# A two-block network on one core: the first projections' chunks five to eight in three passes of halves, and a ninth place for the experts' weights

## The chip, the cores and the metric

The kernel runs on one core of one Trainium2 chip. The metric is the device time of one execution in microseconds. All activations and weights are float32 in HBM.

## The reference, cut to what matters

The network has a first block (a token mixer and a mixture of experts) and a second one (two layers). The change lies in the first projection of the first block and in what surrounds the experts:

```python
hc = modulate(rms_norm(ctx, norm1_g[l]), csh1, csc1)        # 256 context tokens x 1024
s_f, s_b = context_states(hc @ w_in[l][:, HG_KDIM:3 * HG_KDIM + HG_WIDTH], lbs[l])
hx = modulate(rms_norm(x, norm1_g[l]), sh1, sc1)            # 256 tokens x 1024
x_mix, _, _ = token_mixer(hx @ w_in[l], lbs[l], s_f, s_b, *mix_args)
    # split into q, z_f, z_b, v, g (512 columns each), 3 x 512 for the Hyena branch, 2 x 1024 gate logits
x = x + gt1 * x_mix
x = x + gt2 * hier_moe(modulate(rms_norm(x, norm2_g[l]), sh2, sc2), *moe_args)
    # 32 experts, each with w_up, w_gate (1024 x 512) and w_down (512 x 1024)
```

Each direction of the scan needs log f = log(lb + (1 - lb) * sigmoid(z)), its running sums over chunks of 32 tokens, and several exponentials of them. Then follow two transformer layers of the second block.

## The kernel before, in words

One program lays out by hand what each engine does, in order, with semaphores between engines; there is no scheduler. All weights come through SyncE's (SP's) one queue of loads, in the order of the text. A load of 2 MB fills one **place**: the first part of the kernel has a ring of four places (`ring0` to `ring3`), and load number n may start when the semaphore `ring_used` counts n - 3 places given back (`load`, L503). TensorE (PE) gives a place back with the first product behind the last one that read it.

**Two ways to multiply.** `mm` (L651) on float32 operands is one product that the hardware runs in several passes; the trace shows each such product of 256 columns as two records. `mm3` (L659) multiplies rounded halves (type fp32r): high x high, low x high, high x low, three products that each show as one record. For it somebody must make the halves: a copy to fp32r (high), and the difference (low).

**The first projections.** `WIN_ORDER` walks over twelve chunks of 512 columns of `w_in`. The text below calls them chunk one to chunk twelve; in the code they are j = 0 to 11. A chunk has four tiles of 128 output columns, each the sum over eight k. Chunks one to four use `mm3`, their halves made by VectorE (DVE) with a cast and a subtraction of the whole chunk (`split_first`, L2196). Chunks five to eight use plain float32 `mm` of the weights in the ring against `HX`, the float32 tokens in `X`. Behind chunks two to five PE does two products with `ada_w` each (`BEHIND`); each has its own 2 MB load, so 16 loads pass through the ring in this stretch. PE writes the tiles into four banks in turn and may write tile t when ScalarE (ACT) has taken tile t - 4 (`tile_bank`).

**What runs beside it.** When chunk four is done, DVE starts the scan's preparation: `scan_prep(0)`, `scan_prep(1)` (L2246 to L2271: scalings, running sums, differences), then `scan_products(0)` and `(1)` (L2273 to L2285). ACT takes PE's tiles in order and does the exponentials between them: `scan_exps(0)` behind chunk five and `scan_exps(1)` behind chunk six. In `scan_exps(d)` ACT waits for `ctx_arg` (DVE's preparation of direction d), then for `hg_arg`, which DVE gives only behind both preparations, then for `ke_ready`, three products of DVE later. All engines meet at the end of the stage "projected" (`phase_end`), then comes the scan, the Hyena branch, the merge, the router and the experts.

**The experts.** Their 96 loads of 2 MB go to eight places (`eslot`): the ring's four, three in the arena, one in `H`. Expert load c waits until load c - 8 has been used. The first eight are loaded before the first expert is computed: c = 0 to 3 as the ring comes free, 4 to 6 when the stage "merged" is done, 7 when the router's logits are there. PE uses them in the order up and gate of experts 0 and 1, then per pair of experts the up and gate of the next pair and the down of this one.

**GpSimd (POOL)** does little before the experts: sums of squares, and ten small loads through its own queue (`bring`, L1974): the scan's mask, `c_all_2` (1 MB, read only in the second block), the Hyena tables, `ctx_2`, the router's tables, and later `b2`, `b2_mask` and `gup`.

## Time and profile before

| what | value |
|---|---|
| three runs | 1924.07, 1926.45 and 1928.11 us, median 1926.45 |
| the profiled execution | 1924.48 us, of which the span is 1922.5 us |
| PE busy | 1845.1 us (96%) |
| DVE busy | 891.0 us (46%) |
| ACT busy | 604.1 us (31%) |
| POOL busy | 377.5 us (20%) |
| read from HBM | 425.21 MB, 222 GB/s over the span |

Times in the trace count from the span's start. A PE that is busy isn't a PE at its peak, since its products are pipelined: the pitch from start to start tells what one costs. The kernel's own order gives the stages: first projections from 47 to 198 us, the scan to 270, Hyena to 330, merge and router to 392, experts to 865, the second block to the end.

### The profile page before, as it was taken

To read this page: it belongs to the slowest core of one execution; us is meant where nothing else is said; L and a number is where in the kernel's file an instruction comes from. 1 tells how busy PE (TensorE), PEld (TensorE's weight loads), DVE (VectorE), ACT (ScalarE), POOL (GpSimd) and SP (SyncE) were. 2 spreads that over 40 slices of the span, in tenths; PEclk is the share of its full clock that TensorE was granted. 3 is DMA by queue.
4 is the path that set the end of the run, shared out by engine and by line. 5 is a ranking of instruction groups with operands and counts; after the bars stand their busy time and mean duration, and the time that the engine had idled before them with its cause. 6 is when DMAs were issued, how large, how long until landed. Compare 5 with 4: busy or idle time off the path is not lost.

```text
span 1922.5 us, 26155 instructions
## 1 busy us (share of the span) xinstructions
PE 1845.1 (96%) x11140; PEld 1355.4 (71%) x11140; DVE 891.0 (46%) x1475; ACT 604.1 (31%) x898; POOL 377.5 (20%) x191
## 2 busy tenths in 40 slices
PE   8999999999999989899999899999999999899998
PEld 3878887844444434447877667888888788679998
DVE  4435266621111111128786844566655735673333
ACT  4323123221211111123224424223333411554554
POOL 1000000100000000024002032333343160025664
PEclk9999999999999999999999999999999999999999
DMA  9568136589999999964646014454444322414550
GB/s 358 212 236 314 50 148 246 227 367 427 426 428 427 426 427 427 428 278 181 219 164 211 1 35 152 157 191 155 153 153 157 127 91 91 175 67 156 192 194 30
DMA packets 109361, 427.93 MB, mean 223 GB/s; under 512 B 6096, under 2 KB 11616, under 8 KB 96448
## 3 DMA queue, kind: packets, MB, share of 16 engines
q1 hardware_dynamic: 108272, 420.82, 56.5%
q0 software_dynamic: 976, 5.46, 0.8%
q8 instruction: 89, 1.46, 0.3%
q14 instruction: 24, 0.20, 0.0%
HBM read 425.21 MB, written 1.05 MB: 222 GB/s over the span
## 4 chain that ended last, share of the span: by engine, by line
PE 54%; DMA 17%; issue 6%; DVE 5%; PEld 4%; ACT 3%; PEldq 0%; SPq 0%; POOL 0%; ACTq 0%; DVEq 0%; POOLq 0%
PE bank L651 53%; DMA ring<-in_moe_w_down 7%; DMA H<-in_moe_w_down 4%; DMA arena<-in_moe_w_down 4%; PEld bank L651 4%; PE bank L666 1%; DMA arena<-in_hy 0%; DMA ring<-in_w_in 0%; DVE arena L2722 0%; PEldq L486 0%; DVE ring_low L2798 0%; DVE ring_low L2342 0%; DVE ring_low L2792 0%; ACT arena L1482 0%; ACT arena_r L1964 0%
## 5 line engine op out<-in xcount | busy, mean ns | idle before, releaser
L651 PE MATMUL bank<-arena_r,ring_low 128*128 128x512 f32 (+2 forms) x1920 | 594.8, 341 | 4.2 <-issue 3.1
L651 PE MATMUL bank<-arena_r 128*128 128x256 f32 (+1 forms) x2176 | 589.8, 339 | 4.9 <-POOL arena_r L2066 1.8
L651 PEld LDWEIGHTS bank<-arena_r 128*128 128x128 f32 x2176 | 383.4, 190 | 55.7 <-issue 10.1
L651 PEld LDWEIGHTS bank<-arena_r,ring_low 128*128 128x128 f32 (+1 forms) x1920 | 351.1, 188 | 50.5 <-issue 5.6
L651 PE MATMUL bank<-arena 128*128 128x64 bf16 (+7 forms) x2880 | 353.8, 316 | 28.4 <-DMA H<-in_moe_w_down 8.9
L651 PEld LDWEIGHTS bank<-arena 128*128 128x128 bf16 (+4 forms) x2880 | 199.3, 130 | 184.5 <-issue 167.4
L651 PE MATMUL bank<-H_low,arena_r 128*128 128x512 f32 (+1 forms) x672 | 216.9, 340 | 0.0
L2780 DVE SCALAR_TENSOR_TENSOR X<-bank,mod,X 128x256 f32<-128x256 f32 x216 | 94.3, 479 | 194.8 <-PE bank L651 194.8
L651 PE MATMUL bank<-ring,arena 128*64 128x512 f32 x768 | 170.3, 599 | 8.0 <-DMA ring<-in_moe_w_down 8.0
L2053 POOL TENSOR_TENSOR ring_low<-ring,arena_r 128x2048 fp32r<-128x2048 f32 x31 | 142.3, 4612 | 127.8 <-DVE ring_low L2792 67.9
L2519 DVE SCALAR_TENSOR_TENSOR arena_r<-bank,arena,arena_r 128x512 fp32r<-128x512 f32 x32 | 24.0, 751 | 309.1 <-ACT arena_r L1708 309.1
L1513 ACT ACTIVATE arena<-bank 128x512 f32<-128x512 f32 (+2 forms) x106 | 51.0, 495 | 338.8 <-PE bank L651 319.4
L2066 POOL TENSOR_TENSOR arena_r<-arena,arena_r 128x512 fp32r<-128x512 f32 (+1 forms) x64 | 104.6, 1647 | 234.1 <-ACT arena L1946 234.1
L651 PEld LDWEIGHTS bank<-ring,arena 128*64 128x64 f32 x768 | 56.6, 138 | 114.4 <-issue 114.2
L651 PEld LDWEIGHTS bank<-H_low,arena_r 128*128 128x128 f32 x672 | 124.2, 189 | 15.2
L2849 DVE SCALAR_TENSOR_TENSOR arena<-ring,silu_rows 128x1024 f32<-128x1024 f32 x84 | 99.5, 1222 | 65.1 <-POOL arena_r L2066 61.7
L651 PE MATMUL bank<-H,arena 128*64 128x512 f32 (+4 forms) x464 | 116.0, 429 | 8.1 <-DVE arena L2738 2.8
L651 PE MATMUL bank<-X,ring 128*128 128x256 f32 x512 | 117.6, 385 | 0.0
L1939 ACT ACTIVATE arena_r<-ring 128x4096 fp32r<-128x4096 f32 x15 | 54.4, 3630 | 175.7 <-DMA ring<-in_w_mlp 126.7
L651 PEld LDWEIGHTS bank<-X,ring 128*128 128x128 f32 x512 | 96.2, 192 | 15.7 <-issue 3.5
L651 PE MATMUL bank<-H_low,ring_low 128*128 128x512 f32 (+2 forms) x272 | 93.4, 358 | 0.0
L651 PE MATMUL bank<-ring_low,arena_r 128*128 128x512 f32 x288 | 92.8, 394 | 0.6 <-issue 0.6
(334 smaller groups left out, 1929.0 us busy)
## 6 DMA issues: line engine op xcount, KB each, us to landing
ring<-in_w_mlp SPq DMA_DIRECT2D x32, 2048.0 KB, 7.9
ring<-in_w_in SPq DMA_DIRECT2D x25, 2048.0 KB, 8.7
ring<-in_moe_w_up SPq DMA_DIRECT2D x17, 2048.0 KB, 23.3
ring<-in_moe_w_gate SPq DMA_DIRECT2D x17, 2048.0 KB, 28.0
ring<-in_ada_w SPq DMA_DIRECT2D x16, 2048.0 KB, 11.6
arena<-in_moe_w_up SPq DMA_DIRECT2D x15, 2048.0 KB, 22.7
ring<-in_moe_w_down SPq DMA_DIRECT2D x14, 2048.0 KB, 23.3
arena<-in_moe_w_down SPq DMA_DIRECT2D x13, 2048.0 KB, 23.6
```

The lines of the kernel that those rows point to most:

```text
L651: ins = nc.tensor.matmul(o, l, r, start=start, stop=stop, skip_group_check=True)
L666: ins = nc.tensor.transpose(o, i, ident)
L1513: A_(o, i, f, **kw).then_inc(S("tile_free"), 1)
L1939: A_(W2h, slot(n), ACT.Copy).then_inc(S("w_high"), 1)
L2053: G.tensor_tensor(low(n)[:, s], slot(n)[:, s], W1h[:, s].bitcast(F32), ALU.subtract).then_inc(S("w1_split"), 1)
L2066: G.tensor_tensor(HAl[:, nt, 0:W], HA[:, nt, 0:W], HAh[:, nt, 0:W].bitcast(F32), ALU.subtract)\
L2519: V.scalar_tensor_tensor(YSl[:, s], ps[6 + nb][:, :], WSL, YSh[:, s].bitcast(F32), ALU.mult, ALU.subtract)\
L2780: i = V.scalar_tensor_tensor(X[:, t, s * L:(s + 1) * L], o[:, s * L:(s + 1) * L], mod[:, 1 + l, gate + t, s:s + 1], X[:, t, s * L:(s + 1) ...
L2849: d = V.scalar_tensor_tensor(CPROD[:, c, :], as_turned(n)[:, q % 3, :], 1.0, CSIL[:, c, :], ALU.mult, ALU.mult, accum_out=mod[:, 2, bass.d ...
```

## The change

1. Chunks five to eight use `mm3`. The tokens' halves are copied by POOL once into a new 2 MB tensor `spare` (`XHh`, `XHl`). The weights' halves are made in quarters, one per tile: ACT copies a quarter (128 x 8 x 128 values) into `W4h`, one buffer for all four chunks, behind its take of the same tile of the chunk before; POOL subtracts it from the chunk into `ring_low`; PE waits for each quarter (`w_quarter`).
2. `scan_exps` is cut in two. Its later part, now `scan_exps_next(d)`, stands behind the second tile of chunk six (d = 0) and of chunk seven (d = 1).
3. The products with `ada_w` are spread as one, one, two, two, two behind chunks two to six.
4. The loads that POOL issued are issued by ACT; `c_all_2` by SP in the second block, with its Silu on ACT at the start of that block instead of in the middle of the experts.
5. The first expert load has a place of its own, `spare`, which takes no other one. The other 95 go round the eight old places, so load c (from 9) waits for load c - 8 as before; two waits for places at the end of the experts move on by one.

```diff
-        BEHIND = [[], [0, 1], [2, 3], [4, 5], [6, 7], [], [], []]
+        BEHIND = [[], [0], [1], [2, 3], [4, 5], [6, 7], [], []]
...
         def eslot(c):
 
-            s = c % MRING
+            if c == 0:
+                return spare
+            s = (c - 1) % MRING
...
-            return MOE + NMOE - MRING + (n - L0) + 1
+            return MOE + NMOE - MRING + (n - L0) + 2
...
         W0h = [ar_r[:, 8192:12288], ar_r[:, 18432:22528]]
+        W4h = ar_r[:, 19456:23552].rearrange("p (k n) -> p k n", k=KT)
...
-                if c < RING:
-                    sp.wait_ge(used, MOE + c - RING + 1)
-                elif c == RING:
+                if c == 0:
+                    sp.wait_ge(S("phase"), 4 * (PHASES.index("projected") + 1))
+                elif c <= RING:
+                    sp.wait_ge(used, MOE + c - 1 - RING + 1)
+                elif c == RING + 1:
                     sp.wait_ge(S("phase"), 4 * (PHASES.index("merged") + 1))
-                elif c == MRING - 1:
+                elif c == MRING:
                     sp.wait_ge(S("logits"), TB)
-                elif c >= MRING:
+                elif c > MRING:
                     sp.wait_ge(used, MOE + c - MRING + 1)
...
                 def turn_rows(t):
-                    if (j, t) == (5, 1):
+                    if (j, t) == (6, 1):
                         ada_turn(4, 6, 0, 8)
...
-                else:
-                    chunk_in(n)
+                if j == 4:
+                    pe.wait_ge(S("pool_ready"), 2)
...
                 for nt in range(2 if j == 0 else 0, 4):
+                    if j >= 4:
+                        pe.wait_ge(S("w_quarter"), 4 * (j - 4) + nt + 1)
                     o = tile_bank()
...
-                            mm(o[:, 0:L], as_cols(n)[:, k, t], HX[:, k, :], k == 0, k == KT - 1, done)
+                            mm3(o[:, 0:L], (W4h[:, k, t], as_cols(n, slot=low)[:, k, t]), (XHh[:, k, :], XHl[:, k, :]), k == 0, k == KT - 1, done)
...
+            def high_quarter(j, nt):
+
+                n = win(j)
+                act.wait_ge(full[n % RING], arrived(n))
+                t = slice(nt * P, (nt + 1) * P)
+                A_(W4h[:, :, t], as_cols(n)[:, :, t], ACT.Copy).then_inc(S("high_copied"), 1)
+
...
+                    if 4 <= j < 7:
+                        high_quarter(j + 1, nt)
+                    if (j, nt) == (5, 1):
+                        scan_exps_next(0)
+                    if (j, nt) == (6, 1):
+                        scan_exps_next(1)
+                if j == 3:
+                    for nt in range(4):
+                        high_quarter(4, nt)
...
+            G.tensor_copy(XHh, Hp[:, :, 0:L].bitcast(F32)).then_inc(S("pool_ready"), 1)
+            G.tensor_copy(XHl, Hl[:, :, 0:L].bitcast(F32)).then_inc(S("pool_ready"), 1)
+            for j in range(4, 8):
+                n = win(j)
+                for nt in range(4):
+                    t = slice(nt * P, (nt + 1) * P)
+                    pool.wait_ge(S("high_copied"), 4 + 4 * (j - 4) + nt + 1)
+                    G.tensor_tensor(as_cols(n, slot=low)[:, :, t], as_cols(n)[:, :, t], W4h[:, :, t].bitcast(F32), ALU.subtract)\
+                        .then_inc(S("w_quarter"), 1)
             phase_end(pool, "projected")
...
             phase_end(act, "experts")
+            bring(b2t, T["b2"], "b2_in")
+            bring(gmask, T["b2_mask"].rearrange("p (a b) -> p a b", a=2), "b2_in")
+            bring(GUP[0:32, :, :], T["gup"][0].rearrange("d r n -> r d n"), "b2_in")
```

**ACT, chunks six and seven.** These rows of before are ACT's instructions between the last take of chunk five and the last take of chunk six; L1513 takes a tile from its bank, L1581 to L1589 are `scan_exps`.

```order
L1485 ACT_TABLE_LOAD
L1581 ACTIVATE arena<-arena 128x1024 [waits ctx_arg]
L1583 ACTIVATE arena<-arena 128x1024 [waits hg_arg]
L1584 ACTIVATE arena<-arena 128x1024
L1585 ACTIVATE arena<-arena 128x1024
L1587 ACTIVATE arena<-arena 128x1024 [waits ke_ready]
L1589 ACTIVATE chunk_decay<-arena 128x32
L1513 ACTIVATE arena<-bank1 128x256 [waits tile_done]
L1513 ACTIVATE arena<-bank2 128x256 [waits tile_done]
L1513 ACTIVATE arena<-bank3 128x256 [waits tile_done]
L1513 ACTIVATE arena<-bank0 128x256 [waits tile_done]
```

And the same place of the change; L1537 takes a tile, L1624 is the copy of a quarter (of chunk seven, in `ring2`), L1605 the first exponential, L1610 to L1616 are `scan_exps_next(0)`.

```order
L1509 ACT_TABLE_LOAD
L1605 ACTIVATE arena<-arena 128x1024 [waits ctx_arg]
L1537 ACTIVATE arena<-bank1 128x256 [waits tile_done,pool_ready]
L1624 ACTIVATE arena_r<-ring2 128x8x128 [waits full2]
L1537 ACTIVATE arena<-bank2 128x256 [waits tile_done]
L1624 ACTIVATE arena_r<-ring2 128x8x128 [waits full2]
L1610 ACTIVATE arena<-arena 128x1024 [waits hg_arg]
L1611 ACTIVATE arena<-arena 128x1024
L1612 ACTIVATE arena<-arena 128x1024
L1614 ACTIVATE arena<-arena 128x1024 [waits ke_ready]
L1616 ACTIVATE chunk_decay<-arena 128x32
L1537 ACTIVATE arena<-bank3 128x256 [waits tile_done]
```

The exponentials that wait for `hg_arg` and `ke_ready` moved behind two takes and two copies, and each copy waits for the landing of chunk seven's weights (`full2`).

**SP, the loads behind chunk four's weights.** In before, chunk five's weights (`in_w_in` to `ring2`) are followed by two of `ada_w` and chunk six's:

```order
L509 DMA ring2<-in_w_in 128x8x512 [waits ring_used]
L509 DMA ring3<-in_ada_w 128x8x512 [waits ring_used]
L509 DMA ring0<-in_ada_w 128x8x512 [waits ring_used]
L509 DMA ring1<-in_w_in 128x8x512 [waits ring_used]
L509 DMA ring2<-in_w_in 128x8x512 [waits ring_used]
L509 DMA ring3<-in_w_in 128x8x512 [waits ring_used]
```

In the change the same weights, from chunk five's in `ring0` on, lie so:

```order
L522 DMA ring0<-in_w_in 128x8x512 [waits ring_used]
L522 DMA ring1<-in_ada_w 128x8x512 [waits ring_used]
L522 DMA ring2<-in_ada_w 128x8x512 [waits ring_used]
L522 DMA ring3<-in_w_in 128x8x512 [waits ring_used]
L522 DMA ring0<-in_ada_w 128x8x512 [waits ring_used]
L522 DMA ring1<-in_ada_w 128x8x512 [waits ring_used]
L522 DMA ring2<-in_w_in 128x8x512 [waits ring_used]
L522 DMA ring3<-in_w_in 128x8x512 [waits ring_used]
```

Chunk six's weights still stand third behind chunk five's, and now chunk seven's stand third behind chunk six's, where before they followed at once.

## Rows read from the trace of the kernel before

**Rows 1.** The page: the profiled execution's span.
```profile
span 1922.5 us, 26155 instructions
```
**Rows 2.** Busy time by stage: window, length, PE, PEld, DVE, ACT, POOL, clock, DMA share, GB/s.
```profile
134.00:198.00 64.00, 63.64 (x328) 51.13 (x327) 34.63 (x55) 24.17 (x38) 1.29 (x2) 1.00 0.77 281
...
392.00:508.00 116.00, 115.51 (x966) 52.62 (x966) 19.33 (x66) 22.70 (x38) 4.74 (x8) 1.00 0.95 401
508.00:833.00 325.00, 301.94 (x2310) 138.84 (x2306) 49.43 (x150) 50.11 (x89) 0.00 (x0) 0.98 1.01 427
```
**Rows 3.** The chain that ended last: start, length, what.
```profile
508.88 26.23 DMA ring<-in_moe_w_down
```
**Rows 4.** PE's timeline: start, length, group, idle before it and releaser.
```profile
70.98 0.28 PE L651 MATMUL bank<-arena_r 128*128 128x256 f32 x1
...
82.59 1.92 PE L651 MATMUL bank<-ring,silc 128*32 128x512 f32 x16
...
133.89 3.64 PE L651 MATMUL bank<-ring,silc 128*32 128x512 f32 x32
...
162.86 34.78 PE L651 MATMUL bank<-X,ring 128*128 128x256 f32 x160
198.15 1.98 PE L651 MATMUL bank<-arena 128*128 128x512 f32 x4 [0.51 <-ACTq L486]
```
**Rows 5.** ACT's timeline.
```profile
134.49 0.59 ACT L1513 ACTIVATE arena<-bank 128x512 f32<-128x512 f32 x1
...
161.47 1.04 ACT L1585 ACTIVATE arena<-arena 128x1024 f32<-128x1024 f32 x1
166.20 1.06 ACT L1587 ACTIVATE arena<-arena 128x1024 f32<-128x1024 f32 x1 [3.69 <-DVE arena L2283]
...
314.75 3.71 ACT L1655 ACTIVATE arena_r<-ring 128x2048 fp32r<-128x2048 f32 x2 [5.99 <-DVEq L2358]
```
**Rows 6.** DVE's timeline beside chunks five and six.
```profile
134.00 1.67 DVE L2250 TENSOR_SCALAR arena<-arena,lbc 128x512 f32<-128x512 f32 x4 [24.87 <-PE bank L651]
...
154.20 0.42 DVE L2270 TENSOR_TENSOR H<-arena 128x256 f32<-128x256 f32 x1
...
158.25 1.23 DVE L2276 TENSOR_TENSOR arena<-arena 128x1024 f32<-128x1024 f32 x1 [3.63 <-ACT arena L1581]
```
**Rows 7.** POOL's subtractions by form: count, busy, mean ns, idle before.
```profile
L2053 POOL TENSOR_TENSOR ring_low<-ring,arena_r 128x2048 fp32r<-128x2048 f32 x31 | 142.3, 4612 | 127.8 <-DVE ring_low L2792 67.9 <-ACT arena_r L1910 59.9
L2028 POOL TENSOR_TENSOR X<-X 128x512 f32<-128x512 f32 x2 | 2.6, 1287 | 0.2
```
**Rows 8.** The timeline of DVE and POOL where they meet.
```profile
881.17 4.43 DVE L2613 TENSOR_TENSOR ring_low<-ring,ring_low 128x4096 fp32r<-128x4096 f32 x1
881.37 5.38 POOL L2028 TENSOR_TENSOR arena<-arena 128x512 f32<-128x512 f32 x1
885.51 2.32 DVE L2602 SCALAR_TENSOR_TENSOR arena<-arena,silu_rows 128x1024 f32<-128x1024 f32 x1
```
**Rows 9.** SP's issues of loads.
```profile
83.66 2.08 SPq L509 DMA_DIRECT2D ring<-in_ada_w  x2
86.85 1.28 SPq L509 DMA_DIRECT2D ring<-in_w_in  x1
...
421.62 0.33 SPq L563 DMA_DIRECT2D arena<-in_moe_w_up  x1
```
**Rows 10.** Issue to landing in us (last number): the loads issued at 83.66, 86.85 and 421.62 us.
```profile
ring<-in_ada_w SPq DMA_DIRECT2D x1, 2048.0 KB, 7.8
ring<-in_w_in SPq DMA_DIRECT2D x1, 2048.0 KB, 15.4
arena<-in_moe_w_up SPq DMA_DIRECT2D x1, 2048.0 KB, 10.4
```
**Rows 11.** The start of the second block, ACT's and POOL's timelines.
```profile
866.04 0.61 POOL L1975 DMA_DIRECT2D arena<-in_b  x1 [5.16 <-DVEq L486]
...
866.51 0.91 ACT L1499 ACTIVATE arena_r<-H,mod 128x256 fp32r<-128x256 f32 x2 [1.31 <-DVE H L2111]
```

More of the change, by code:

```diff
@@ L191, in build @@
             ar = shared("arena", [P, AR])
+            spare = shared("spare", [P, KT * 512])[:, :]
         ring_r = [sb(f"ring_low{s}", [P, KT * 512], F32R) for s in range(RING)]
@@ L196, in build @@
         ar_r = sb("arena_r", [P, AR], F32R)
+        spare_r = sb("spare_r", [P, KT * 512], F32R)[:, :]
+        XHh, XHl = [spare_r[:, KT * L * a:KT * L * (a + 1)].rearrange("p (k n) -> p k n", k=KT) for a in range(2)]
+        CSIL = spare[:, 0:2 * D].rearrange("p (a d) -> p a d", a=2)
         ps = [ctx.enter_context(nc.psum_tensor(f"bank{b}", [P, 512], F32))[:, :] for b in range(8)]
@@ L605, in _ @@
                     load(first + 2 * j, cols(T["w_in_2"][l], j * 512, 512), as_cols(first + 2 * j))
+                    if l == 0 and j == 1:
+                        sp.dma_start(CSIL, T["c_all_2"].rearrange("p (a d) -> p a d", a=2)).then_inc(S("rows_in"), 16)
                 if l == 0:
@@ L1039, in rows @@
                 for c in (cu, cu + 1):
-                    pe.wait_ge(full[c % MRING], earrived(c))
+                    expert_in(pe, c)
                 up, gate = [eslot(c).rearrange("p (k n) -> p k n", k=KT) for c in (cu, cu + 1)]
@@ L1066, in expert_pair @@
                 for c in (cd, cd + 1):
-                    pe.wait_ge(full[c % MRING], earrived(c))
+                    expert_in(pe, c)
                 w = [eslot(c).rearrange("p (k n) -> p k n", k=4) for c in (cd, cd + 1)]
@@ L1468, in _, with bring @@
             A_ = nc.scalar.activation
+            def bring(dst, src, sem):
+                act.dma_start(dst, src).then_inc(S(sem), 16)
+            tall = lambda a: a.rearrange("(k p) n -> p k n", p=P)
             own = [0]
@@ L1581, in scan_exps, with scan_exps_next @@
                 A_(KM[d], KM[d], ACT.Exp).then_inc(S("ctx_exp"), 1)
+            def scan_exps_next(d):
                 act.wait_ge(S("hg_arg"), d + 1)
@@ L1611, in _ @@
                     gate_log(d)
-                if j == 4:
+                if j == 5:
                     ada_rows(4, 6, 0)
@@ L1618, in _ @@
                     scan_exps(1)
+            act.wait_ge(S("ada_turned"), 5)
+            bring(hmask, T["hg_mask"].rearrange("p (a b) -> p a b", a=2), "tables_in")
             phase_end(act, "projected")
@@ L1629, in _ @@
             phase_end(act, "scan_b")
+            bring(A(15360, 2048), T["hy"], "tables_in")
             for b in range(2):
@@ L1665, in _ @@
             phase_end(act, "hyena")
+            bring(X[:, :, L:2 * L], tall(T["ctx_2"]), "b2_in")
+            bring(mtab, T["moe"], "tables_in")
+            bring(WR, tall(T["wr"]), "tables_in")
             merge_high(3)
@@ L1723, in _ @@
                 expert_pair(p)
-                if p == 2:
-                    act.wait_ge(S("rows_in"), 16)
-                    A_(CSIL, CSIL, ACT.Silu).then_inc(S("silu_c"), 1)
             act.wait_ge(S("passes_known"), 1)
@@ L1789, in _ @@
                     chunk_high(1)
+                    act.wait_ge(S("rows_in"), 32)
+                    A_(CSIL, CSIL, ACT.Silu).then_inc(S("silu_c"), 1)
                 for j in range(8):
@@ L1966, in _ @@
                     mean_root(7, L)
+                if l == 0:
+                    bring(GUP[0:32, :, :], T["gup"][1].rearrange("d r n -> r d n"), "b2_in")
                 phase_end(act, f"l{l}_mlp")
@@ L1972, in _ @@
             G = nc.gpsimd
-            def bring(dst, src, sem):
-                pool.dma_start(dst, src).then_inc(S(sem), 16)
             added = [0]
```

50 lines of the change are left out of this document (23 added, 27 removed).

## The prediction

> **What bounds the kernel now.** I read the windows by stage first. In the first projections PE is busy for 63.6 of 64 us at the full clock of 2.4 GHz [rows 2], and the chain there is PE's own work. From 392 to 508 us PE is still never idle. From 508 to 833 us it idles for 23 us while the DMA engines stand at 1.01 of their share and 427 GB/s: the experts' loads bound it, and the chain of waits says the same with links of 26 us on the landing of a `w_down` [rows 2, 3]. So a microsecond taken from PE in the projections counts in full, if the engines that feed it keep up. A load less for the experts counts if the loads never run dry.
>
> **The products themselves.** The last 160 records of the plain form stretch from 162.86 us to 197.6 us (PE's next group at 198.15 waited 0.5), a pitch of 0.217 us; the four chunks are 256 records, 55.6 us. Chunk two is the new form exactly, 256 columns in three passes: 96 records from 70.98 to 82.59, 0.121 us each, 2.9 us for a tile, 11.6 for a chunk. So 384 records cost 46.4 us: **minus 9.2 us** with full supply [rows 4].
>
> **Who supplies a quarter.** ACT's copy: two of 2048 values take 3.71 us, so 1024 take 0.93 [rows 5]. POOL's subtraction: 4.61 us for 2048 values, so 2.3 for a quarter [rows 7], against a tile of 2.9. That fits, but only just, and three things stand in its way.
>
> *The first quarter.* `W4h` lies on chunk four's high half, so ACT copies only when chunk four is done. Two of the products with `ada_w` now stand behind it instead of before it (3.6 us for two, rows 4): chunk four ends at 130.3, PE is free at 133.9. ACT's last take ends 1.2 us after the chunk [rows 4, 5], the copy 0.9 later, the subtraction 2.3 later: 134.7. PE idles **0.9 us**.
>
> *The weights' landing.* A place is given back when PE starts its next work; SP issued 1.1 us after that (82.59 to 83.66). The first load of three landed 7.8 us after its issue, at 91.5, the third at 102.3: 5.4 us a load [rows 4, 9, 10]. Chunk six's weights are third in such a row. It starts at 130.3 + 1.1, so they land at 139.1 + 2 x 5.4 = 149.9. Before, PE read them only from 155. Now ACT wants them at 140, for the first quarter behind its first take of chunk five, and stands there 9 us. Copy, subtraction and a wait of POOL bring quarter one to 153.7, where PE, without waiting, would be ready at 149.9: **3.8 us** of idle. Chunk seven's weights are third of the next row, that starts when chunk five is done: 146.3 + 1.1 + 7.8 + 10.8 = 166.0; quarter at 169.6, PE ready at 168.7: **0.9 us**, and ACT again stands until 166.
>
> *The exponentials.* `scan_exps_next(0)` stands behind the second copy for chunk seven, so it cannot start before 168.3. It is three exponentials of 1.0, three products of DVE with 3.7 us of waiting, and 1.3 us more: 8 us [rows 5]. Only then come the take and the copy for the third quarter, and the subtraction: 3.6 us.
>
> **VectorE and GpSimd at one port.** At 881.17 DVE began a subtraction of two SBUF tensors of 4.43 us. POOL's, begun 0.2 later, took 5.38 us where its like takes 1.29; and DVE's next, begun at 885.51 when POOL had its turn, took 2.32 [rows 7, 8], about 1.1 over the usual. So they run one after the other and in turn. Nearly all that DVE does from 134.0 to 158 is of that kind, with hardly a gap [rows 6]; POOL was idle then. Now 36.8 us of POOL's subtractions (16 x 2.3) lie there. DVE's two preparations take 20.6 us (134.0 to 154.6). Four quarters of chunk five, four of six and two of seven fall into them and push them by 2.3 each: they begin at 130.3, and end not at 151 but at about 173.5. `hg_arg` comes at 174.8, the exponentials are done at 182.7 (8 us), the third quarter at 186.3. PE has done two tiles of chunk seven by 175.5: **10.8 us** of idle. Direction 1 goes the same way in chunk eight: DVE's first product waits for POOL's subtraction and ends at 189.8; three exponentials, a wait for the port, three products, the rest, copy and subtraction: 203. PE is ready for its third tile at 198.3: **4.7 us**. Two tiles later, at about 209, the stage ends, where before it ended at 197.6 to 198.1.
>
> The Trainium skill says the same in SBUF — State Buffer, Who interferes with whom: a VectorE instruction with two SBUF inputs and a GpSimd one that reads SBUF take the shared port pair in turns, whoever comes first for the whole instruction. By that rule the sum stands as above; without it the idle times of the next part hold. The trace agrees in the one place that rows 8 show.
>
> **Sum for the projections**: idle 0.9 + 3.8 + 0.9 + 10.8 + 4.7 = 21.1, less 9.2, is 11.9; from the ends by laying the work out it is 11. I take **plus 11.3**.
>
> **Bounds of it.** If the port cost nothing, `hg_arg` is there before ACT: exponentials 168.3 to 176.3, quarter at 179.9, PE ready at 175.5: 4.4, and 2.7 in chunk eight: 12.7 of idle less 9.2, plus 3.5, or plus 1.7 when laid out from the ends. If only the sixteen running sums don't use the port, plus 4.6. If POOL must wait until DVE has a gap, chunk five starts at about 152, but then DVE is done and later quarters come in time: plus 8 to 9. If a quarter in its strided form costs 2.6 us, plus 15.
>
> **The ninth place.** Load 12 is the tightest: issued at 421.62, landed 10.4 us later where a load with a free queue takes 7.8 [rows 9, 10]. One load fewer ahead of it brings it 2.6 us forward and no more, since it waits for PE to use load 4, and PE there is bound by itself [rows 2]. So **minus 2.6 us**; bounds 0 and one whole load, 2.1 MB at 427 GB/s, 4.9.
>
> **ACT's new issues.** An issue took 0.33 on SP and 0.6 on POOL [rows 9, 11]. The mask's stands before the meeting at the end of the projections, the Hyena tables' before the first copies of that stage, `gup`'s before the last meeting of layer 0: 0.4 each. Three stand before the shifts at 866.5, 1.5 us, of which about 0.6 lies in ACT's wait for DVE [rows 11]; PE waits for the first shifts. Together **plus 2.1**, bounds 0.5 and 4. The three behind Hyena stand before a copy that isn't wanted for 20 us, `c_all_2`'s Silu lies in a wait of ACT for PE's first tiles: nothing. If that cover is gone, 3 us.
>
> **PE's clock** was full in the whole stretch [rows 2]; with an idle of 11 us it may fall to the 1.2 GHz level for a tile or two: 0 to 2, I take **0.5**, for the later wait hides part.
>
> Sum: 11.3 - 2.6 + 2.1 + 0.5 = **plus 11.3 us**. The profiled execution took 1924.5 (span 1922.5 [rows 1] and 2.0 around it), so 1935.8; it lay 2.0 below the median, to which the same sum gives 1937.8. I say 1937.
>
> **The rivals.**
> - *The port does no harm*, since the turns are finer than rows 8 suggest. Then plus 1.7 with 2.1 + 0.0 - 2.6: 1927.7. For it speaks that only one clear meeting is in my rows. With the running sums outside the port: 1930.5. Together 0.22.
> - *It becomes faster*: PE gets each quarter in time and the 9.2 us stay, with 2.6 of the place less 2.1 of issues: 1916.7. It decides at one point: chunk six's weights must be in by 145 instead of 149.9, and chunk seven's by 160, with the port free. The landings in rows 10 speak against it. 0.10.
> - *The third pass does not help*: a record of 256 columns costs more than 0.121 beside quarters that are strided. Chunk two speaks against it, which had the same weight shape. It would add 1 us per 0.003 of pitch and lies in the range.
> - *As forecast*, the port in turns or in DVE's favour, 1933 to 1943: 0.63. Worse than that, up to 1948: 0.05.
>
> **Chances.** The measurement tells about 0.2%, 4 us, from no change. Faster by more: 0.10 and a little of the first rival, 0.11. Within 4 us: part of the first rival, 0.12. Slower: 0.77. The range takes in the forecast and the first rival, 1927 to 1943, and leaves out the faster case, half of what lies at 1927 and the tail.
>
> **What would show it.** In the changed profile: PE's tiles at 2.9 us; an idle before chunk six of 3 to 4 us and before the third tile of chunk seven of about 10, both ended by POOL's subtraction; running sums of DVE that take 2.9 instead of 0.7 us; ACT idle for some 9 us twice on a landing of `w_in`; PE's first group of the scan at about 209.5 instead of 198.15; load 12 landing about 2.6 us nearer to the scan's start than now. If DVE's instructions keep their lengths, the step on the port is wrong, and the first rival holds; if PE has no idle of over 2 us before 200, the landings are wrong too and the kernel is faster.

## The result, and the profile after

The changed kernel takes 1934.73 us (median of eight runs, 1930.81 to 1947.49); the kernel before took 1923.67 in the same measurement (1921.33 to 1929.94). The ratio is 1.0059, with a 95% interval of 1.0038 to 1.008: about 11 us slower. The profiled execution took 1933.14 us.

The page's first line, as [rows 1]:

```profile
span 1931.4 us, 26455 instructions
```

The windows by stage, to be held against [rows 2]; the columns are the same:

```profile
134.00:198.00 64.00, 54.78 (x412) 48.75 (x408) 52.79 (x49) 34.20 (x48) 37.63 (x15) 0.89 0.88 319
392.00:508.00 116.00, 115.66 (x953) 55.36 (x953) 26.16 (x102) 22.39 (x44) 4.85 (x8) 0.98 0.93 385
508.00:833.00 325.00, 305.04 (x2334) 140.13 (x2332) 49.41 (x150) 50.43 (x89) 0.00 (x0) 0.98 1.01 427
```

In the 64 us of the projections PE was busy for 63.6 and is now for 54.8, and its granted clock there fell from 1.00 to 0.89. The experts' stretch is the same, bound by DMA. So the projections are where the time went. PE's timeline there (start, length, group, idle before it and releaser), beside [rows 4]:

```profile
130.41 3.64 PE L668 MATMUL bank<-ring,silc 128*32 128x512 f32 x32
135.63 0.48 PE L668 MATMUL bank<-spare_r,arena_r 128*128 128x256 f32 x2 [1.58 <-issue]
...
155.11 0.80 PE L668 MATMUL bank<-spare_r,arena_r 128*128 128x256 f32 x2 [4.16 <-POOL ring_low L2048]
...
181.88 1.89 PE L668 MATMUL bank<-base,mod_rows 128*128 128x16 f32 x8 [2.91 <-ACT mod_rows L1541]
...
199.01 0.50 PE L668 MATMUL bank<-spare_r,arena_r 128*128 128x256 f32 x2 [1.58 <-POOL ring_low L2048]
205.76 0.70 PE L668 MATMUL bank<-arena 128*128 128x512 f32 x1 [0.73 <-ACTq L499]
```

PE waits 1.58 us before chunk five (the profile names no releaser, but POOL's first subtraction ended at 135.53, 0.1 before), 4.16 before chunk six, 2.91 before the turn of the `ada_w` rows behind the second tile of chunk seven, 1.58 before the third tile of chunk eight. The scan's first group starts at 205.76, where it was 198.15: plus 7.6. ACT's timeline, beside [rows 5]:

```profile
151.39 1.06 ACT L1624 ACTIVATE arena_r<-ring 128x1024 fp32r<-128x1024 f32 x1 [10.06 <-DMA ring<-in_w_in]
...
167.71 1.06 ACT L1624 ACTIVATE arena_r<-ring 128x1024 fp32r<-128x1024 f32 x1 [6.63 <-DMA ring<-in_w_in]
177.70 1.06 ACT L1614 ACTIVATE arena<-arena 128x1024 f32<-128x1024 f32 x1 [4.87 <-DVE arena L2333]
186.04 1.06 ACT L1610 ACTIVATE H<-H 128x1024 f32<-128x1024 f32 x1 [0.84 <-DVEq L2328]
194.08 1.06 ACT L1614 ACTIVATE H<-arena 128x1024 f32<-128x1024 f32 x1 [5.08 <-DVE arena L2333]
```

L1624 is the copy of a quarter: ACT stands 10.06 us for the weights of chunk six and 6.63 for those of chunk seven. L1610 to L1614 are the exponentials; the wait for three products of DVE was 3.69 us [rows 5] and is now 4.87 and 5.08. DVE and POOL, beside [rows 6, 7]:

```profile
132.71 0.67 DVE L2307 TENSOR_TENSOR_SCAN arena<-base,arena 128x256 f32<-128x256 f32 x1
133.29 2.79 DVE L2306 TENSOR_TENSOR_SCAN arena<-base,arena 128x256 f32<-128x256 f32 x1
136.00 2.83 DVE L2307 TENSOR_TENSOR_SCAN arena<-base,arena 128x256 f32<-128x256 f32 x1
...
132.63 11.14 POOL L2048 TENSOR_TENSOR ring_low<-ring,arena_r 128x1024 fp32r<-128x1024 f32 x4 [67.68 <-ACT arena_r L1624]
152.52 10.73 POOL L2048 TENSOR_TENSOR ring_low<-ring,arena_r 128x1024 fp32r<-128x1024 f32 x4 [8.75 <-ACT arena_r L1624]
168.85 5.34 POOL L2048 TENSOR_TENSOR ring_low<-ring,arena_r 128x1024 fp32r<-128x1024 f32 x2 [5.60 <-ACT arena_r L1624]
```

A running sum takes 0.67 us with POOL idle and 2.8 beside a quarter of POOL's, so it waits 2.1 us. A subtraction takes 2.4 us where DVE is idle and 2.8 beside the sums. Each sum is followed by one subtraction and each subtraction by one sum: each engine gets one instruction done in about 2.75 us.

**The way of the 8.9 us of span.** From the projections' first product to the scan's first group: 151.0 us before, 158.55 now, plus 7.5. From there to ACT's last copies of the experts' outputs: 658.0 and 657.1, minus 0.9, in which PE has 6.8 us at half clock near 390 us where before it had 3.4. From there to the first shifts of the second block: 10.35 and 10.98, plus 0.6. Behind them: plus 1.6, and this part does not lie in the work: up to DVE's last instruction it is minus 0.3, and the last of the four stores of the output then lands 4.1 us after its issue, where before it took 2.15. In nine of the fourteen profiles of this document that store takes 3.6 to 4.4 us, in five (before, `plain`, `filler`, `port_load`, `issues`) 2.15. The change's own kernel and `filler` differ by eight products of PE alone and fall on either side, so I don't count these 2.0 us as an effect of the change; their cause is open.

### The profile page after: what moved, and what is told of

Read it like the earlier page. It is cut to its first block, busy times and chain, and to the rows that moved or that the text cites. A ratio compares the mean times of both kernels' runs of the same rounds, so it can differ in the third digit from the quotient of the medians.

```text
span 1931.4 us, 26455 instructions
## 1 busy us (share of the span) xinstructions
PE 1841.9 (95%) x11268; PEld 1358.6 (70%) x11268; DVE 915.8 (47%) x1475; ACT 618.8 (32%) x914; POOL 421.2 (22%) x199
## 4 chain that ended last, share of the span: by engine, by line
PE 55%; DMA 15%; PEld 4%; DVE 4%; ACT 3%; issue 3%; PEldq 0%; SPq 0%; ACTq 0%; POOL 0%; DVEq 0%
PE bank L668 54%; DMA arena<-in_moe_w_down 9%; DMA ring<-in_moe_w_down 6%; PEld bank L668 4%; PE bank L683 1%; DMA arena<-in_hy 0%; DMA ring<-in_w_in 0%; DVE arena L2773 0%; PEldq L499 0%; DVE ring_low L2849 0%; DVE ring_low L2393 0%; DVE ring_low L2843 0%; ACT H L1517 0%; ACT arena L1506 0%; ACT arena_r L2017 0%
## 5 line engine op out<-in xcount | busy, mean ns | idle before, releaser
L668 PE MATMUL bank<-ring,arena 128*64 128x512 f32 x768 | 259.1, 606 | 13.6 <-DMA arena<-in_moe_w_down 8.0
L668 PEld LDWEIGHTS bank<-ring,arena 128*64 128x64 f32 x768 | 81.0, 139 | 123.0 <-issue 122.8
L1537 ACT ACTIVATE arena<-bank 128x512 f32<-128x512 f32 (+2 forms) x106 | 51.3, 495 | 318.6 <-PE bank L668 298.6
L2900 DVE SCALAR_TENSOR_TENSOR arena<-ring,spare 128x1024 f32<-128x1024 f32 x84 | 99.5, 1222 | 64.9 <-POOL arena_r L2116 61.5
L668 PE MATMUL bank<-H,arena 128*64 128x512 f32 (+4 forms) x448 | 107.1, 418 | 11.5 <-DMA ring<-in_moe_w_down 3.4
L668 PEld LDWEIGHTS bank<-H,arena 128*64 128x64 f32 (+2 forms) x448 | 48.8, 174 | 65.1 <-issue 59.3
```

The costliest lines, as they stand in the source:

```text
L668: ins = nc.tensor.matmul(o, l, r, start=start, stop=stop, skip_group_check=True)
L1537: A_(o, i, f, **kw).then_inc(S("tile_free"), 1)
L2900: d = V.scalar_tensor_tensor(CPROD[:, c, :], as_turned(n)[:, q % 3, :], 1.0, CSIL[:, c, :], ALU.mult, ALU.mult, accum_out=mod[:, 2, bass.d ...
```

## The experiments

All numbers called "the stage" run from the projections' first product to the scan's first group on PE. That start itself lay between 46.6 and 52.3 us in the profiled executions of kernels that are the same up to it. PE's idle time is the sum of all gaps in the stage.

| kernel | ratio to before (95%) | stage, us | PE idle in it | PE's clock, 125 to 210 us |
|---|---|---|---|---|
| before | 1 | 151.0 | 0.7 | 1.00 |
| the change | 1.0059 (1.0038 to 1.008) | 158.5 | 11.0 | 0.92 |
| plain | 0.9996 (0.9979 to 1.0012) | 151.0 | 0.8 | 1.00 |
| eight | 1.0063 (1.0039 to 1.0087) | 158.5 | 11.4 | 0.92 |
| port | 1.0012 (0.9995 to 1.003) | 155.7 | 8.2 | 0.92 |
| loads | 1.0071 (1.0043 to 1.0098) | 164.8 | 20.9 | 0.90 |
| exps | 1.0056 (1.0037 to 1.0076) | 157.2 | 10.5 | 0.92 |
| loads_exps | 1.0081 (1.0059 to 1.0102) | 162.5 | 18.8 | 0.90 |
| loads_port | 0.9987 (0.9969 to 1.0005) | 147.3 | 4.3 | 0.98 |
| loads_exps_port | 0.9972 (0.9957 to 0.9987) | 142.9 | 1.6 | 1.00 |
| inter | 0.997 (0.9958 to 0.9983) | 143.5 | 2.3 | 1.00 |
| filler | 1.0059 (1.0036 to 1.0081) | 161.2 | 9.4 | 0.96 |
| port_load | 1.0059 (1.0039 to 1.0078) | 160.1 | 8.1 | 0.96 |
| issues | 1.001 (0.9989 to 1.0032) | 151.0 | 0.8 | 1.00 |

**The theory** is the prediction's: the quarters come late, through weights that land late, through exponentials in front of ACT's copies, and through DVE and POOL in turns at one port. Its rivals: one of the three alone does it, or the lower clock does.

### plain and eight: the parts apart

`plain` sets the projections back and keeps the ninth place and the issues; `eight` keeps the projections and takes the ninth place away.

```diff
 # plain, core of it
-                            mm3(o[:, 0:L], (W4h[:, k, t], as_cols(n, slot=low)[:, k, t]), (XHh[:, k, :], XHl[:, k, :]), k == 0, k == KT - 1, done)
+                            mm(o[:, 0:L], as_cols(n)[:, k, t], HX[:, k, :], k == 0, k == KT - 1, done)
 # eight, core of it
-            s = (c - 1) % MRING
+            s = c % MRING
```

> The changed kernel with its first projections set back to plain float32 products (parts 1 to 3 of the change undone; the ninth place and the moved issues stay). The sum of the prediction says: minus 2.6 us for the ninth place, plus 2.1 us for ScalarE's issues, so minus 0.5 us against the kernel before. The trace of the changed kernel suggests that the issues cost less, about 1 us, so minus 1.6. Rival: a place more is worth nothing, since the loads are the bound and their number is the same: plus 1 to 2. Second rival: it is worth a whole load, minus 4.9 plus the issues, so about minus 3. In the trace: PE's wait before the last pair of experts comes 2.6 us earlier than at 833.15 if the first holds, not earlier if the rival does, 4.9 earlier if the second does.

> The changed kernel with the experts' weights on eight places again (part 5 undone; the halves, the moved issues and the 2 MB tensor for the tokens' halves stay). If the ninth place is worth 2.6 us, it is 2.6 us slower than the changed kernel, 1937.3 us or a ratio of 1.0072 to the kernel before. If it is worth nothing, 1934.7 (1.0059). If it is worth a whole load, 1939.6 (1.0085). The scan's start stays at 205.8 in all cases.

`plain` measures the same as before, and its stage is the old one to 0.01 us: within the interval, which is 3 us wide to either side, the loss lies in parts 1 to 3. The profiled execution of `plain` had a mean clock of 0.87 in the 64 us from 206 us on, so its wait before the last pair of experts can't be read as expected. The stage of `eight` is that of the change; the scan started at 210.8 instead of 205.8 only because the projections began 5.0 us later. Its ratio lies 0.0004 above the changed kernel's, too little for its interval. The traces tell it: from the first product that gathers the experts' tokens to ACT's last copies of their outputs take 463.4 us (before), 462.8 (issues), 461.9 (port_load) and 461.6 (eight) with eight places, and 459.0 to 461.1 in nine profiles with nine places, but 462.8 in the tenth (`filler`). The means are 462.4 and 460.2: **about 2.2 us** for the place. It is a mean and no more: the two groups overlap, and single pairs give anything from 0.7 (`eight` and the change) to 3.7 us (`issues` and `plain`). Load 12 lands 7.5 us after its issue now (10.4 in [rows 10]).

### port, loads, exps: one cause taken away at a time

```diff
 # port
-                    G.tensor_tensor(as_cols(n, slot=low)[:, :, t], as_cols(n)[:, :, t], W4h[:, :, t].bitcast(F32), ALU.subtract)\
-                        .then_inc(S("w_quarter"), 1)
+                    G.memset(as_cols(n, slot=low)[:, :, t].bitcast(F32), 0.0)
+                    pool.drain()
+                    G.memset(as_cols(n, slot=low)[:, :, t].bitcast(F32), 0.0).then_inc(S("w_quarter"), 1)
 # loads
-        BEHIND = [[], [0], [1], [2, 3], [4, 5], [6, 7], [], []]
+        BEHIND = [[], [0, 1], [2, 3], [4, 5], [], [6, 7], [], []]
 # exps (and the turn of the ada rows at (6, 3))
-                    if (j, nt) == (5, 1):
+                    if (j, nt) == (5, 3):
                         scan_exps_next(0)
-                    if (j, nt) == (6, 1):
+                    if (j, nt) == (6, 3):
                         scan_exps_next(1)
```

> The changed kernel with GpSimd's quarter subtraction replaced by two fills with zero of the same quarter of ring_low, one after the other. They read no SBUF. It leaves out the low halves of the weights of chunks five to eight: PE multiplies by zeros there, with the same number of products. If GpSimd's reading and VectorE's instructions with two SBUF inputs take the port in turns, the running sums fall from 2.8 to 0.67 us, both preparations end by about 156 us, ScalarE's two waits for three products of VectorE fall from 5 to 3.7 us, and the scan's first group on PE comes 3 to 6 us earlier than at 205.8. If the landings of the weights and the place of the exponentials alone set the stage, VectorE's instructions get shorter but the scan's first group moves by less than 1.5 us. If there is no contention the lengths stay at 2.8 us.

> The changed kernel with the ada_w products (and so their loads) spread as two, two, two, none, two behind chunks two, three, four, five and six, so that the weights of chunk six are the first of their row of loads to land and those of chunk seven too. By the landings of the trace chunk six's weights come at 139 us instead of 150 and chunk seven's at 155 instead of 166; ScalarE's waits of 10.1 and 6.6 us for them go. If the landings cost what the trace of the changed kernel suggests, PE's 4.2 us of idle before chunk six go and the scan's first group comes 4 to 6 us earlier, about 1930 us in all. If the port is the bound, what is gained before chunk six is given back before the third tiles of chunks six and seven, since VectorE's preparation now meets GpSimd all the time and ends near 173: the scan's first group moves by less than 2 us, 1933 to 1935.

> The changed kernel with the later part of the exponentials two tiles later, behind the fourth tile of chunks six and seven instead of the second, and PE's turn of the ada rows behind the fourth tile of chunk seven. From the first product of the projections to the scan's first group it is 151.0 us before, 158.5 after. If the place of the exponentials holds the third quarters up, the 2.9 us of idle in chunk seven and 1.6 in chunk eight go, the stage takes 154 to 155 us and the time is about 4 us below the changed kernel's. If the landings and the port set the pace and the exponentials are only where the wait shows, the stage stays within 1 us of 158.5.

In the timeline of `port` the running sums are back at 0.67 us beside POOL's fills, which only write SBUF:

```profile
137.67 0.95 POOL L2048 MEMSET ring_low<- 128x1024 f32 x1 [67.62 <-ACT arena_r L1624]
...
137.78 0.67 DVE L2308 TENSOR_TENSOR_SCAN arena<-base,arena 128x256 f32<-128x256 f32 x1
138.36 0.67 DVE L2307 TENSOR_TENSOR_SCAN arena<-base,arena 128x256 f32<-128x256 f32 x1
...
181.59 1.06 ACT L1614 ACTIVATE arena<-arena 128x1024 f32<-128x1024 f32 x1 [3.69 <-DVE arena L2334]
```

The stage falls by 2.9 us, just under the lowest that the theory expected. ACT's two waits for DVE gave back 2.6 (4.87 and 5.08 to 3.69 each), and its wait of 0.84 for `hg_arg` went too. The edit is not the port alone: two fills take 2.0 us where a subtraction took 2.4 alone and 2.8 beside DVE, so each quarter is also ready 0.4 to 0.9 us sooner behind its copy, and up to that much of the 2.9 can be due to it. The total fell by more than that, 0.0047 of the ratio, about 9 us; the intervals of the two ratios leave the difference open between some 4 and 14.

`loads` did the opposite of what was expected. The weights came in time (ACT waited 2.42 us instead of 10.06 and 6.63), and the stage grew by 6.3:

```profile
159.66 1.06 ACT L1624 ACTIVATE arena_r<-ring 128x1024 fp32r<-128x1024 f32 x1 [2.42 <-DMA ring<-in_w_in]
160.62 0.37 ACT L1537 ACTIVATE arena<-bank 128x256 f32<-128x256 f32 x1
160.88 1.05 ACT L1624 ACTIVATE arena_r<-ring 128x1024 fp32r<-128x1024 f32 x1
176.74 1.06 ACT L1610 ACTIVATE arena<-arena 128x1024 f32<-128x1024 f32 x1 [14.80 <-DVEq L2328]
...
135.39 22.75 POOL L2048 TENSOR_TENSOR ring_low<-ring,arena_r 128x1024 fp32r<-128x1024 f32 x8 [71.02 <-ACT arena_r L1624]
```

POOL now makes eight quarters in one row and two more behind them, all ten beside DVE's preparation; DVE finishes it at 175.4, ACT stands 14.8 us for `hg_arg` in front of its copies, and PE 16.4. That is the picture that the prediction had drawn for the change itself. In the change the late weights kept POOL away from DVE: eight subtractions met the preparation.

But the edit moves a second thing. It puts two more products with `ada_w` in front of chunk four's end, as in the kernel before, and DVE's preparation waits for that end. Counted from the first product, the preparation starts 3.4 us later than in the change (133.28 less 46.61 against 130.52 less 47.21) and ends 7.7 later. So 3.4 of these 7.7 us are the place of the `ada_w` products and only 4.3 are two more turns at the port; the 6.3 us of stage can't all be put down to weights that are early.

`exps` moves the stage by 1.3 us. ACT makes the four quarters of chunk seven first, so POOL's four subtractions now lie beside DVE's products, and ACT waits 6.74 and 7.18 us for these where it waited 4.87 and 5.08. PE's idle time in chunk seven is gone, and 3.92 us of it stand before chunk eight. Its ratio is that of the changed kernel.

### Two and three causes together

The same edits combined; in the kernels with `port` the low halves are left out.

> Both: the loads of chunks six and seven first in their rows, and the exponentials behind the fourth tiles. GpSimd still makes the low quarters. The loads alone made the stage 164.8 us, since VectorE's preparation met GpSimd at the port all the way to 175 us and the exponentials waited for it. If it is the wait for the exponentials through which the port costs time, most of these 16 us of idle go, since the quarters of chunk seven no longer stand behind them: the stage takes 149 to 153 us, the time is near 1925 or below. If the port holds up the quarters themselves, it stays above 158.

> The same with two fills with zero in place of each low quarter (the low halves of chunks five to eight are left out). The case of full supply: weights early, port free, exponentials out of the way. Then the 9.2 us of the products should show whole: a stage of 142 to 145 us, PE at full clock in it, and a total 9 to 12 us below the kernel before (ninth place minus 2.5, issues plus 1). If the third pass itself costs more in this place than in chunk two, or the half clock comes without idle, the stage stays above 148.

> The changed kernel with the weights of chunks six and seven first in their rows of loads and with two fills with zero in place of each low quarter (low halves left out); the exponentials stay behind the second tiles. The stage took 158.5 us in the changed kernel, 155.7 with the fills alone, 164.8 with the loads alone, 142.9 with both and the exponentials moved. If the two causes were late weights and the port, and the place of the exponentials hardly matters once both are gone, the stage takes 143 to 147 us. If the exponentials' place is a cause of its own, it takes 150 or more.

`loads_exps` came out 10 us above the 149 to 153 that were expected, on the side of its rival: the copies of chunk seven no longer stand behind the exponentials, but the turn of the `ada` rows does (in ACT's order it comes after them), and ACT waited 16.68 us for `hg_arg`. `loads_port` gives 147.3, all three edits 142.9, with PE at full clock. So the three causes aren't a sum: from 158.5, `port` alone brings 2.9, `loads` alone costs 6.3, both bring 11.2, and the third edit then brings 4.5 more, where alone it brought 1.3. The port shows its full weight where the weights are early: with them the fills bring 17.5 us (164.8 to 147.3), without them 2.9. With full supply the products' 9.2 us show almost whole: 151.0 less 9.2 is 141.8.

### port_load: POOL's work without PE waiting for it

```diff
 # in the kernel before, on POOL; flat is the 128 x 2 x 1024 tensor for the second block's rows,
 # filled with zero earlier (that line is left out here)
+            pool.wait_ge(S("tile_done"), 16)
+            for i in range(8):
+                G.tensor_tensor(flat[:, 1, :], flat[:, 0, :], flat[:, 0, :], ALU.subtract)
+                pool.drain()
```

> The kernel before with work on GpSimd that nobody waits for: eight subtractions of 128 x 1024 values of two SBUF operands into the scratch of the second block's rows, from the end of chunk four on. If GpSimd and VectorE take the port in turns, VectorE's running sums last 2.8 us instead of 0.67, its preparation ends at about 172 instead of 154.6, ScalarE's exponentials behind chunk five wait until then and hold its takes of PE's tiles up, and the scan's first group comes 8 to 14 us later than at 151.0 us from the first product. If VectorE's longer instructions have enough slack here, the sums get longer but the stage stays within 2 us of 151. If there is no contention, nothing changes.

```profile
133.58 8.33 DVE L2257 TENSOR_SCALAR arena<-arena,lbc 128x512 f32<-128x512 f32 x4 [24.68 <-PE bank L651]
141.83 2.38 DVE L2263 TENSOR_TENSOR_SCAN arena<-base,arena 128x256 f32<-128x256 f32 x1
...
133.62 16.74 POOL L1995 TENSOR_TENSOR silu_rows<-silu_rows 128x1024 f32<-128x1024 f32 x8 [73.83 <-PE bank L651]
...
168.86 1.06 ACT L1583 ACTIVATE arena<-arena 128x1024 f32<-128x1024 f32 x1 [11.13 <-DVEq L2285]
...
177.11 29.36 PE L651 MATMUL bank<-X,ring 128*128 128x256 f32 x128 [7.51 <-ACT arena L1513]
```

That is the timeline of DVE, POOL, ACT and PE in turn. Eight subtractions, one every 2.1 us, that nobody waits for cost the kernel before 9.1 us of stage. DVE's four scalings take 8.33 us instead of 1.67 [rows 6], four sums 2.3 instead of 0.67; the preparation ends at 167.5, ACT waits 11.13 us for it and takes no tiles, and PE finds its banks full for 7.51 us. PE's idle time grew by 7.4 us; the other 1.7 of the 9.1 come mostly from 6.8 us at half clock that begin in this wait.

### filler: the clock apart from the waits

```diff
+                    if (j, nt) == (5, 0):
+                        keep_busy(7, 4)
+                    if (j, nt) == (7, 2):
+                        keep_busy(7, 1)
...
                     if (j, t) == (6, 1):
+                        keep_busy(7, 3)
```

> The changed kernel with seven plain products of 512 columns on the identity, into a bank that nobody reads, where PE idled: four before the first tile of chunk six, three before the turn of the ada rows in chunk seven, and an eighth before the third tile of chunk eight. They add nothing to the result. If PE's two stretches at half clock come from its idle time and cost what they last (6.8 us each, so 3.4 lost in each), they go and the stage takes 152 to 155 us. If the stage is set by ScalarE's chain (weights at 167, exponentials, copies), the clock's loss lies in front of waits that grow by as much: the granted clock rises to 1.0 in the stage, and the stage stays at 158 to 159 us.

PE's windows (only PE is asked: length, busy, clock, DMA share, GB/s), first of the changed kernel:

```profile
155.00:160.00 5.00, 4.89 (x23) 0.50 1.05 387
...
185.00:190.00 5.00, 5.00 (x32) 0.67 0.71 262
200.00:205.00 5.00, 5.00 (x42) 1.00 0.00 0
```

and of `filler`:

```profile
155.00:160.00 5.00, 5.00 (x43) 1.00 1.05 387
...
185.00:190.00 5.00, 5.00 (x44) 1.00 0.22 52
200.00:205.00 5.00, 5.00 (x26) 0.52 0.00 0
```

PE's timeline of `filler` at the third tile of chunk eight:

```profile
198.73 0.80 PE L668 MATMUL bank<-spare_r,arena_r 128*128 128x256 f32 x2 [3.62 <-POOL ring_low L2053]
```

With work in the idle stretches the clock stays at 2.4 GHz where it had been at the 1.2 GHz level, and the third tile of chunk eight starts at 198.73 instead of 199.01 (the projections having begun 0.3 earlier): nothing is gained. The faster PE only waits longer, 3.62 us instead of 1.58. At the end of that wait the clock falls (6.8 us at the 1.2 GHz level from 198.0 on), now with no wait left to hide it, and the last two tiles cost 2.7 us more. So the stage of the changed kernel is set by ACT's chain, not by the clock. The expectation had named this case with a stage of 158 to 159 us, but not the loss behind it: the stage took 161.2.

### issues: ACT's issues alone

```diff
 # the kernel before; nine such lines leave POOL, at the changed kernel's places on ACT
+            def bring(dst, src, sem):
+                act.dma_start(dst, src).then_inc(S(sem), 16)
```

> The kernel before with nine of the ten small loads issued by ScalarE instead of GpSimd, at the places where the changed kernel has them (c_all_2 stays on GpSimd). By the prediction's term it costs 2.1 us, bounds 0.5 and 4; by the trace of the changed kernel less, 0.2 to 0.4 at the scan's start and about 1 before the first shifts of the second block, so plus 1 to 1.5 us. If it lies wholly in waits, nothing.

The ratio is 1.001, not to be told from 1. In the trace the stage is the old one, and the way from ACT's last copies to the first shifts is 10.99 us instead of 10.35, as in the changed kernel:

```profile
867.88 0.35 ACTq L1471 DMA_DIRECT2D arena<-in_b  x1
868.26 0.46 ACTq L1471 DMA_DIRECT2D arena<-in_b_mask  x1
868.75 0.45 ACTq L1471 DMA_DIRECT2D arena<-in_gup  x1
869.25 0.91 ACT L1504 ACTIVATE arena_r<-H,mod 128x256 fp32r<-128x256 f32 x2 [1.95 <-DVE H L2119]
```

Of 1.3 us for the three issues, half lies in ACT's wait for DVE. So the trace shows **0.6 us** at this place and nothing in the stage; the ratio's interval would allow 6 us in all.

### inter: a version that beats both

All arithmetic of the changed kernel, the loads of `loads`, but DVE makes the low quarters itself, between the parts of its preparation, the exponentials are cut in two where they wait, and the turn of the `ada` rows stands behind the fourth tile of chunk seven. So it shows that such a version exists, not what each of its edits is worth.

```diff
                     prep_scale(0)
+                    low_quarters(4, 0, 4)
                     prep_sums(0)
+                    low_quarters(5, 0, 2)
                     prep_mids(0)
+                    low_quarters(5, 2, 4)
                     products_a(0)
...
 # ACT, chunk six: the second tile's take, then
+                    if (j, nt) == (5, 1):
+                        scan_exps_a(0)
 # ACT, behind chunk six's last copies
+                    scan_exps_b(0)
```

> With all arithmetic: the loads as in the two before, but VectorE makes the low quarters itself, two or four at a time between the parts of its preparation, in the order in which PE needs them (1.2 us for each instead of 2.4 on GpSimd, and nobody at the port beside it); the exponentials of each direction are cut into a part that waits for VectorE's sums and one that waits for its products. Laid out from the rows of the other runs: the stage takes 142 to 146 us, the time is 6 to 12 us below the kernel before, about 1916. If VectorE becomes the bound (its instructions sum to about 58 us of the 71 from chunk four's end), PE idles before quarters that end late: a stage of 148 to 152 us and a time within 3 us of the kernel before.

```profile
136.06 4.63 DVE L2300 TENSOR_TENSOR ring_low<-ring,arena_r 128x1024 fp32r<-128x1024 f32 x4 [0.39 <-ACT arena_r L1627]
140.60 0.68 DVE L2315 TENSOR_TENSOR_SCAN arena<-base,arena 128x256 f32<-128x256 f32 x1
...
160.25 1.06 ACT L1627 ACTIVATE arena_r<-ring 128x1024 fp32r<-128x1024 f32 x1 [1.63 <-DMA ring<-in_w_in]
```

The timeline shows DVE's first four quarters, its sums at 0.67 us behind them, and ACT's longest wait for weights. PE's window of the stage (length, busy, clock, DMA share, GB/s):

```profile
125.00:210.00 85.00, 82.76 (x642) 1.00 0.65 235
```

A quarter costs DVE 1.16 us, where on POOL it took 2.4 to 2.8 and held DVE up for 2.1. The stage is 143.5 us, the kernel 0.3% faster than before (interval 0.17 to 0.42%), some 17 us below the change as it stands. The median fell by 5.8 us and the profiled span by 8.8 (with 1.9 more in the last store's landing), where 6 to 12 had been expected.

## Why the prediction was right, point by point

- **The sum.** Plus 11.3 was foreseen; measured were plus 11.1 in the medians and plus 8.9 in the two profiled spans. The direction and the chain of causes were right; that the size met so closely is in good part luck. With the clock's 0.5 the stage was to grow by 11.8 us and grew by 7.5; the issues were to cost 2.1 and show 0.6; 2.0 us of the spans lie in the landing of the last store, which the prediction doesn't have, and another 2.2 of the medians in no term.
- **The products.** The third pass costs what chunk two says: `loads_exps_port` ends the stage 8.1 us early with 1.0 more of idle, so 9.1 for the products, and `inter`, with true low halves, 7.5 early with 1.6 more, so 9.2. The rival of a dear third pass is ruled out.
- **Chunks five and six.** 0.9 and 3.8 foreseen, 1.58 and 4.16 measured, by the same chains: chunk six's weights landed just before 151.4, where 149.9 stood in the prediction.
- **Chunk seven, the term that was mis-sized.** "10.8 us of idle" before its third tile, from DVE's preparation ending at 173.5. Measured: 2.9. The landing foreseen at 166.0 came at 167.7, but I had counted two of chunk seven's quarters into the preparation although they can't begin before the weights are there. The preparation ended at 168.3 by itself, with eight subtractions in it instead of ten, before ACT got to the exponentials at 169.9. `loads` showed the drawn picture where the weights are early. And the wait showed elsewhere: at the turn of the `ada` rows, whose copy stands in ACT's order behind the same exponentials.
- **Chunk eight.** Third quarter at 203, measured 199.0, since direction 1 followed the earlier end of direction 0: its first product with DVE, foreseen to end at 189.8, ended at 186.0. PE was ready at 197.4, where 198.3 was foreseen, in spite of its half clock. So 1.6 of idle instead of 4.7; at full clock (`filler`) it is 3.6 with the quarter at the same time.
- **The stage as added up.** Foreseen were 21.1 us of idle and 0.5 for the clock, less 9.2 for the products. Measured: idle grew by 10.4, and the 13.7 us at half clock cost PE some 6.2 (an estimate: half of their length outside the waits); less 9.2 that is 7.4, where the stage shows 7.5.
- **The port.** Turns, as foreseen: 2.8 us for a sum. This was argued from one meeting [rows 8] and is shown now by `port` and `port_load`. Its weight in the sum was overrated: 2.9 us by `port`, where the two cases of the prediction lay 9.6 apart. With the weights early it would have been underrated (17.5 us). The Trainium skill (SBUF — State Buffer, Who interferes with whom) says that a VectorE instruction with two SBUF inputs contends with a GpSimd one that reads SBUF and not with one that only writes; the traces agree on both: 2.79 us beside the subtractions, 0.67 beside the fills.
- **The rival that was faster.** Its conditions, weights by 145 and 160 and a free port, gave 3.7 of the 9.2 us with the exponentials in their place (`loads_port`: 147.3); with all three it came out at a ratio of 0.9972, 5 us below the kernel before (the prediction had 9.7 for it), with the low halves left out.
- **The ninth place**: minus 2.6 foreseen, minus 2.5 in the profiled pair and about minus 2.2 in the means, with a spread as large. That load 12 would land 2.6 us nearer to the scan's start did not show (1.3): the experts' first product comes 1.6 us later behind the scan's start, and the half clock near 390 us lies between; from its issue it is 2.9.
- **ACT's issues**: plus 2.1 foreseen, 0.6 found in the trace, before the second block's first shifts. Nothing of them is seen in the stage; at Hyena and in layer 0 I did not measure them apart.
- **The clock**: 0.5 was foreseen in the stage. There it costs nothing by itself, as `filler` shows; the two stretches of 6.8 us at half clock lie in front of waits. Outside it the profile has 3.4 us more at half clock near 390 us, which cost 1.7.

Open: of the 11.1 us of the medians the profiled pair shows 8.9, 2.0 of them in the last store's landing, whose cause is not known. The other 2.2 can be a lower clock: the mean over the eight executions of the changed kernel is 0.983, in its profiled one 0.985. That is not shown.

## What to carry to other kernels

When an idle engine is given work, ask who shares a port with it and who waits for that neighbour: eight subtractions that nobody needed cost 9 us here, through VectorE and ScalarE. Before crediting a faster step, lay out its supply chain in the order of each engine; with several causes in one chain, removing one can do little (`port`) or make it worse (`loads`, in part through what else its edit moves), and only all together show the gain. A slow stretch in front of a wait is free, the same stretch behind the last wait is not, so look at what ends the stage before summing losses.

## What the runs showed that I had not expected

- The clock of one and the same kernel varies between executions, and the time with it: the kernel before took 1920.66 us at a mean granted clock of 0.992 and 1935.69 at 0.980, about 1.2 us for each thousandth. Kernels whose PE idles in the projections mostly have the lower ones (means 0.981 to 0.984 for exps, loads_exps, loads, eight and port, 0.988 for before), though filler and port_load, with 9.4 and 8.1 us of idle, have 0.987 and 0.986.
- DVE's scaling of one SBUF tensor by a column (TENSOR_SCALAR, 128x512) also waits for POOL: 8.33 us for four instead of 1.67.
- The first projections begin between 46.6 and 52.3 us in kernels that are alike up to there; in the late ones PE's clock was 0.78 in the first 47 us, in the kernel before 0.96.
